# Input contractions of a streaming encoder layer as three products of rounded pairs, with the weights passed through four slots

## The reference

```python
def _layer(x, pool_hist, cache_k, cache_v, cache_kidx, pos0, rel_bias, g_pre, w_in, w_pool, pool_scale, w_out, g_post):
    h = _rmsnorm(x, g_pre)                                   # 1024 channels
    proj = jnp.einsum('bld,de->ble', h, w_in)                # 2600 columns
    u_a, gate_a, q, k, v, qi, ki, wi, gate_b = jnp.split(proj, _SPLITS, axis=-1)
    y_a, new_pool = _pool_mixer(u_a, pool_hist, pos0, w_pool, pool_scale)
    ...
    y_b = _dsa_attention(q, qi, wi, k_all, v_all, ki_all, pos0, rel_bias)   # top-256 keys by indexer score
    mixed = jnp.concatenate([y_a * jax.nn.silu(gate_a), y_b * jax.nn.silu(gate_b)], axis=-1)
    out = jnp.einsum('ble,ed->bld', mixed, w_out)
    return x + _rmsnorm(out, g_post), k, v, ki, new_pool
```

## Time and profile before

| | |
|---|---|
| median of three runs | 1680.02 us |
| span of the profiled execution, first to last instruction | 1677.7 us |
| TensorE busy | 1556.8 us, 93% |
| VectorE busy | 1214.6 us, 72% |
| ScalarE busy | 892.7 us, 53% |
| GpSimd busy | 474.5 us, 28% |
| DMA over the span | 120.76 MB, mean 72 GB/s |

### The profile page before, as it was taken

One profiled execution on the slowest core, in us unless ns is written; L12 is line 12 of the kernel. 1 busy time (PEld: TensorE's weight loads), 2 busy tenths in 40 slices (PEclk: granted clock), 3 DMA queues, 4 the chain that ended last, 5 costly groups with the idle time before them and its releaser, 6 DMA issues.

```text
span 1677.7 us, 17799 instructions
## 1 busy us (share of the span) xinstructions
PE 1556.8 (93%) x5191; PEld 869.7 (52%) x5191; DVE 1214.6 (72%) x2940; ACT 892.7 (53%) x1684; POOL 474.5 (28%) x384
## 2 busy tenths in 40 slices
PE   7999899989999999896988898999999999999996
PEld 4555555555555887663444444444444444455552
DVE  5412578779897566675469999999998999985322
ACT  3112333343334455451498988898988776523331
POOL 0111211121113132303343443434323342322241
PEclk9999999989999999987998999999999999999999
DMA  9322322221112111078324211221220220201011
GB/s 366 74 42 49 80 61 71 56 82 40 61 42 70 48 50 37 35 222 253 81 63 120 80 50 57 59 85 39 61 76 26 52 63 1 63 25 26 32 34 49
DMA packets 91979, 120.76 MB, mean 72 GB/s; under 512 B 17150, under 2 KB 63806, under 8 KB 91499
## 3 DMA queue, kind: packets, MB, share of 16 engines
q1 hardware_dynamic: 90506, 115.44, 22.1%
q10 hardware_dynamic: 1376, 4.19, 2.2%
HBM read 76.06 MB, written 43.54 MB: 71 GB/s over the span
## 4 chain that ended last, share of the span: by engine, by line
PE 23%; DVE 18%; ACT 6%; issue 5%; POOL 2%; POOLq 0%; DVEq 0%; ACTq 0%
PE wide L1648 7%; PE wide L1633 7%; DVE above L345 6%; DVE max_junk L1711 3%; ACT act_junk L1542 2%; PE bank L1613 2%; PE bank L1614 2%; PE bank L1615 2%; PE bank L1618 2%; POOL E L1501 1%; PE bank L1599 1%; DVE den L1727 1%; ACT E L1576 1%; DVE reach L383 1%; DVE S L379 1%
## 5 line engine op out<-in xcount | busy, mean ns | idle before, releaser
L931 PE MATMUL bank<-hT,home 128*128 128x512 f32 (+2 forms) x1280 | 486.1, 516 | 5.1 <-DVE sga L1145 2.4
L1501 POOL TENSOR_TENSOR E<-E,home 128x512 f32<-128x512 f32 (+1 forms) x174 | 251.9, 1452 | 446.8 <-ACT E L1576 446.7
L931 PEld LDWEIGHTS bank<-hT,home 128*128 128x128 f32 x1280 | 234.8, 191 | 165.1 <-issue 144.0
L1576 ACT ACTIVATE E<-bank 128x512 f32<-128x512 f32 (+1 forms) x290 | 165.5, 571 | 245.1 <-PE bank L1618 243.3
L1633 PE MATMUL wide<-E,home 128*128 128x512 f32 x544 | 285.1, 606 | 9.9 <-POOL E L1501 9.7
L907 ACT ACTIVATE relu<-wide 128x1024 f32<-128x1024 f32 (+7 forms) x192 | 153.9, 802 | 216.7 <-PE wide L949 154.5
L1183 DVE SCALAR_TENSOR_TENSOR S<-relu,wi,S 128x1024 f32<-128x1024 f32 (+7 forms) x168 | 173.7, 1034 | 100.1 <-ACT relu L907 92.6
L1711 DVE CUSTOM_DVE_ANT_0 max_junk<-bank,mask 128x512 bf16<-128x512 f32 (+3 forms) x230 | 136.9, 615 | 69.2 <-PE bank L1599 54.6
L1648 PE MATMUL wide<-home 128*128 128x512 f32 x272 | 142.2, 614 | 23.2 <-ACT osb L1568 23.0
L1542 ACT ACTIVATE act_junk<-S,minus_cand 128x1152 bf16<-128x1152 f32 (+5 forms) x105 | 155.4, 1480 | 1.5
L949 PE MATMUL wide<-kiT,qiT 96*128 96x512 f32 (+3 forms) x304 | 139.4, 527 | 6.6 <-ACT relu L907 6.5
(11 more groups left out here) (204 smaller groups left out, 2392.2 us busy)
## 6 DMA issues: line engine op xcount, KB each, us to landing
xs<-x_prompt SPq DMA_DIRECT2D x16, 512.0 KB, 4.5
home<-w_in SPq DMA_DIRECT2D x16, 512.0 KB, 12.8
xr<-x_prompt SPq DMA_DIRECT2D x16, 512.0 KB, 4.2
y_prompt<-osb SPq DMA_DIRECT2D x16, 512.0 KB, 2.9
first_q<-q_high_scratch SPq DMA_DIRECT2D x24, 256.0 KB, 5.0
s_scratch<-S SPq DMA_DIRECT2D x11, 512.0 KB, 2.7
first_q<-q_low_scratch SPq DMA_DIRECT2D x18, 256.0 KB, 4.2
gb<-gb_scratch SPq DMA_DIRECT2D x17, 256.0 KB, 5.3
```

The source lines that it names most:

```text
L931: mm = pe.matmul(out, stationary(c), moving(c), start=(c == 0), stop=(c == DC - 1))
L1501: pool.tensor_tensor(E[:, k % 4, :, 0:n], E[:, k % 4, :, 0:n], EB[:, kv * GRP:(kv + 1) * GRP, off:off + n], ALU.mult)\
L1576: act.activation(E[:, k % 4, :, 0:n], banks[2 + k % 2][:, 0:GRP * n].rearrange("p (j n) -> p j n", j=GRP), ACT.Exp).then_inc(fl_free, 1)
```

## The change

`contract` does three float32r products for each row block instead of one float32 product: every operand x is kept as a pair, HI (x rounded to float32r) and LO (x minus HI), and HI·LO, LO·HI and HI·HI are summed in PSUM.

For that, ScalarE writes the HI half of hT and VectorE subtracts it from the transposed tile in PSUM to give LO; the bank is free after the second. ScalarE's next copy out of banks 0 and 1 waits for VectorE (`low_parts`). ScalarE also scales and rounds the token-major weights, VectorE computes their LO.

The pairs need twice the room, so the 16 groups no longer stay in SBUF. A `ring` of four slots holds a pair each (1 MB). In the first of four token blocks (`SUPERS`: tiles 0-3, 4-7, 8-11, and 16,12,13,14,15) each group is loaded raw (512 KB), scaled on VectorE (WS), rounded on ScalarE (WS), completed on VectorE (WL), and the pair is stored to a DRAM scratch `w_dram`; in each of the other three blocks it is loaded from there (1 MB). A slot's load waits for the end of the contraction that used it before, and in the first block for the slot's store.

The order changes with it: the sample tile comes first in the last block, where each group is used for two sub-blocks of 288 and 256 columns, and the scores are spread evenly over its contractions. TM of a block's first tile moves ahead of the transposes of its fourth tile. The pool windows of the last block are taken once for both sub-blocks, and PL comes two contractions after its window. The first S tile, `wout`, `ma` and `gpost` go into other places of SBUF in phase 2, and two scratch outputs become U8.

```diff
+SUPERS = [(0, (0, 1, 2, 3), (0,)), (4, (4, 5, 6, 7), (1,)), (8, (8, 9, 10, 11), (2,)), (12, (16, 12, 13, 14, 15), (3, 4))]
+SLOTS = 4
+    def split_weights(done):
+        for _ in range(min(done + 3, 16) - (16 - len(raw))):
+            steps.append(("WS", *raw.pop(0)))
+        for _ in range(min(done + 2, 16) - (16 - len(halved))):
+            steps.append(("WL", *halved.pop(0)))
...
+                    if j == 2 and not first:
+                        seek()
+                        project(("TM", t), 3)
...
+    steps += [("H", ST), ("N", 14)]
+    project(("TM", ST), 2)
...
+    steps += [("H", 12), ("N", 15), ("H", 13)]
     spread(100)
+    project(("TM", 12), 0)
...
+    steps += [("H", 14), ("H", 15), ("HIST",)]
...
+                def load_group(n):
+                    slot = n % SLOTS
+                    v, kind, g = fills[n]
+                    if n >= SLOTS:
+                        end = fill_ends[n - SLOTS]
+                        if end in fa:
+                            sp.wait_ge(fa_full, fa[end] + 1)
+                        else:
+                            sp.wait_ge(fg_full, fg[end] + 1)
+                        if n - SLOTS < 16:
+                            sp.wait_ge(wg_out[slot], 16 * ((n - SLOTS) // SLOTS + 1))
+                    if v == 0:
+                        sp.dma_start(raw_group(slot), A["w_in"][:, i * GROUP:(i + 1) * GROUP]).then_inc(wg_in[slot], 16)
+                    else:
+                        sp.dma_start(ring_split[:, slot].rearrange("p a n -> p (a n)").bitcast(F32), w_dram[:, k])\
+                          .then_inc(wg_in[slot], 16)
...
+                    if s in ends_fill and ends_fill[s] + SLOTS < len(fills):
+                        load_group(ends_fill[s] + SLOTS)
...
+                    elif s[0] == "WL":
+                        sp.wait_ge(wg_low, k + 1)
+                        sp.dma_start(w_dram[:, k], ring_split[:, k % SLOTS].rearrange("p a n -> p (a n)").bitcast(F32))\
+                          .then_inc(wg_out[k % SLOTS], 16)
...
+                low_parts = {fa[x] for x in steps if x[0] == "Q"} | {fa["H", t, i] for t in range(NT) for i in range(2)}
...
-                            act.activation(hT[:, 4 * half:4 * half + 4, tt:tt + P],
+                            act.activation(hT[:, HI, 4 * half:4 * half + 4, tt:tt + P],
                                            banks[k % 2][:].rearrange("p (c n) -> p c n", c=4), ACT.Copy)\
-                               .then_inc(fa_free, 1)
+                               .then_inc(h_high, 1)
...
+                    elif s[0] == "WT":
+                            act.activation(wt[:, HI, c, :], wt_raw[:, c, :], ACT.Copy, scale=gpre[:, c:c + 1])\
+                    elif s[0] == "WS":
+                        act.activation(ring_split[:, k % SLOTS, HI], raw_group(k % SLOTS), ACT.Copy).then_inc(wg_high, 1)
...
-                        mm = pe.matmul(out, stationary(c), moving(c), start=(c == 0), stop=(c == DC - 1))
+                        pe.matmul(out, stationary(HI, c), moving(LO, c), start=(c == 0), stop=False)
+                        pe.matmul(out, stationary(LO, c), moving(HI, c), start=False, stop=False)
+                        mm = pe.matmul(out, stationary(HI, c), moving(HI, c), start=False, stop=(c == DC - 1))
...
+                    elif s[0] == "H":
+                        for half in range(2):
+                            dve.wait_ge(h_high, transposed)
+                            dve.tensor_tensor(hT[:, LO, 4 * half:4 * half + 4, tt:tt + P],
+                                              banks[fa["H", t, half] % 2][:].rearrange("p (c n) -> p c n", c=4),
+                                              hT[:, HI, 4 * half:4 * half + 4, tt:tt + P].bitcast(F32), ALU.subtract)\
+                               .then_inc(fa_free, 1)
...
+                    elif s[0] == "WL":
+                        dve.wait_ge(wg_high, k + 1)
+                        dve.tensor_tensor(ring_split[:, k % SLOTS, LO], raw_group(k % SLOTS),
+                                          ring_split[:, k % SLOTS, HI].bitcast(F32), ALU.subtract).then_inc(wg_low, 1)
```

More of the change, by code:

```diff
@@ L24 @@
 I32 = mybir.dt.int32
+U8 = mybir.dt.uint8
 U32 = mybir.dt.uint32
@@ L127, in phase1_steps, with pool_part @@
     windows, short = [], []
-    def pool_part():
-        while windows:
-            steps.append(("PD", *windows[0]))
-            short.append(("PL", *windows.pop(0)))
+    def pool_part(step=None):
+        for window in windows:
+            window[0] -= 1
+        while windows and windows[0][0] == 0:
+            short.extend(("PL", b, g) for b, g in windows.pop(0)[1])
+        if step is not None and step[0] == "U" and step[1] != SUPERS[-1][2][0]:
+            _, b, g = step
+            steps.append(("PD", b, g))
+            windows.append([2, [(x, g) for x in (SUPERS[-1][2] if b == SUPERS[-1][2][1] else (b,))]])
     def transposes(t):
@@ L143, in scores @@
         return [("I", t, h, c) for c in range(len(score_chunks(t))) for h in range(NIH)] if t >= TOPK // P else []
-    for b, (t0, nt) in enumerate(BLOCKS):
-        last = b == len(BLOCKS) - 1
-        ahead = [] if last else list(range(t0 + nt, t0 + nt + min(3, BLOCKS[b + 1][1])))
-        todo = [(k, b, g) for k, g in (LAST_ORDER if last else FIRST_ORDER)]
-        for i in range(nt):
-            t = t0 + i
+    for v, (_, tiles, subs) in enumerate(SUPERS[:-1]):
+        t0, nt, first = tiles[0], len(tiles), v == 0
+        ahead = list(SUPERS[v + 1][1][:3])
+        todo = [(k, subs[0], g) for k, g in FIRST_ORDER]
+        done = 0
+        for i, t in enumerate(tiles):
             if i == 0:
@@ L173, in phase1_steps @@
             for j, step in enumerate(mine):
-                scale(2)
+                if first:
+                    split_weights(done)
                 if step[0] != "Q":
                     seek()
-                project(step, sum(taking[j:]) if taking[j] else 0)
-                pool_part()
-                if step[0] == "U":
-                    windows.append(step[1:])
-                if step in (("GB", len(BLOCKS) - 1, 2), ("GB", len(BLOCKS) - 1, 3)):
-                    steps.append(("NP", step[2] - 2))
+                project(step, sum(v >= 2 or s[0] == "Q" for s in mine[j:]) if v >= 2 or step[0] == "Q" else 0)
+                done += 1
+                pool_part(step)
                 if j == 0:
@@ L205, in phase1_steps @@
                     steps.append(seeking.pop(0))
+    subs = SUPERS[-1][2]
+    todo = [(k, b, g) for g in range(NG) for k in ("U", "GA") for b in subs]
+    todo += [(k, b, g) for g in range(NG) for k in ("GB", "Q") for b in subs]
+    steps += [("H", ST), ("N", 14)]
+    seek()
+    project(("TM", ST), 2)
+    transposes(ST)
+    pool_part()
+    steps += [("H", 12), ("N", 15), ("H", 13)]
     spread(100)
+    seek()
+    project(("TM", 12), 0)
     pool_part()
+    settle()
+    transposes(12)
+    steps += [("H", 14), ("H", 15), ("HIST",)]
+    pending += scores(ST)
+    unscored = [12, 13, 14, 15]
+    for i, t in enumerate((12, 13, 14, 15)):
+        if i:
+            while pending and pending[0][1] == (ST, 12, 13)[i - 1]:
+                spread(1)
+            seek()
+            project(("TM", t), len(todo) + 1)
+            pool_part()
+            transposes(t)
+        for j in range(LAST_SHARES[i]):
+            step = todo.pop(0)
+            if step[0] != "Q":
+                seek()
+            left = len(todo) + 4 - i
+            total = len(pending) + sum(len(scores(u)) for u in unscored)
+            project(step, len(pending) / min(-(-total // left), len(pending)) if pending else 0)
+            pool_part(step)
+            if j == 1:
+                settle()
+                pending += scores(unscored.pop(0))
+            if step in (("GB", subs[1], 2), ("GB", subs[1], 3)):
+                steps.append(("NP", step[2] - 2))
+    spread(100)
+    while windows:
+        pool_part()
     settle()
@@ L1342, in phase2 @@
         vx_set = sem("vx_set")
-        S_in = [loaded["S_in0"], sem("S_in1"), sem("S_in2")]
+        S_in = [sem(f"S_in{i}") for i in range(3)]
         S_used = sem("S_used")
```

358 lines of the change are left out of this document (199 added, 159 removed).

## The result

The changed kernel takes **1749.32 us** (median of 4 runs, 1747.75 to 1750.55) against 1680.14 for the kernel before: a ratio of 1.0412, 95% interval 1.0397 to 1.0426. The forecast was 1654 and faster.

A forecast was written before the change was run, and what follows sets the result against it. TensorE was taken as the bound, with VectorE rising beside it. Terms -104 + 16 + 11.5 + 26 + 19 + 5 = -26.5 gave 1651.2 from the profiled 1677.7, plus 2.3: 1654 us; its own range 1636 to 1670.

The forecast's parts named there:

- start: Before block 0's first projection: rounding, norms and subtractions in series delay it from 25.67 to 41.5 us, +16 us.
- block 0: First block's contractions: cheaper products gain 25 us, nothing given back, since loads and VectorE's subtractions lie beside TensorE.
- block 1 with its start: Second block: 26 us gained, less 5.5 at the boundary and 6 from VectorE and TensorE being level, leaving 14.5.
- block 2 with its start: Third block: VectorE's load and boundary waits give 189 us, so the whole 26 us gain is given back.
- last block with its start: Last five tiles: gain 27 less 19 for TensorE's idle time, first projection 52 us after the block begins; net 8.
- rest, phase 2: Phase 1 ends one weighted sum and store later, +2; TensorE starts cold after gaps, +3; phase 2 zero or 2 us.
- the products: Contractions: three float32r products of 512 columns take 0.695 us against 0.86; gross gain 104 us with the narrow ones.
- Rival 4: Contractions: the operand load does not hide behind running products, +397 us, 2077 us; chance 0.05.
- rival 3: Block 0: the weight feed sets the pace below 275 GB/s; at 201 it adds 64 us, 1718 us; chance 0.17.
- Rivals 1 and 2: Blocks after block 0: TensorE stays the bound, 1624 us, chance 0.16; or VectorE takes all gains, 1676 us, chance 0.14.
- Rival 2: VectorE takes all but block 0; blocks 1, 2 and the last gain nothing, 1676 us; chance 0.14.

The follow-up runs named there:

- e10: e9 with the scaling and rounding of the token-major weights moved after tile 0's transposes instead of after its norm: 1689.07 us.
- e4: Changed kernel with only HI times HI computed, the other two of the three products left out: 1688.16 us.
- e8: Changed kernel with VectorE's weighted sums of the score heads after the first taking only half of the columns: 1718.11 us.
- e1: Changed kernel with the x loads of tiles 7 to 16 issued by ScalarE instead of by SyncE behind its weight loads: 1736.53 us.
- e3: Changed kernel with blocks 1 to 3 loading only 128 of the 2048 columns of each stored pair: 1726.34 us.
- e13: e12 with blocks 1 to 3 loading only 128 of the 2048 columns of each stored pair: 1662.67 us.
- e11: Changed kernel with the norm that waits for a late x tile moved after the transposes of tiles whose x is already there: 1725.86 us.
- e5: Changed kernel where ScalarE's copy of a transposed half no longer waits until VectorE has subtracted the half before: 1739.79 us.
- e12: Changed kernel with all four edits together, those of e1, e2, e5 and e11: 1684.16 us.
- e14: e12 without a search piece ahead of TM of tiles 4, 8, 16 and 12; the pieces come later: 1673.46 us.
- e2: Changed kernel with the last block's contractions ordered U,GA,U,GA and GB,Q,GB,Q over the two sub-blocks instead of U,U,GA,GA: 1722.37 us.
- e15: e14 with tiles 14 and 15 transposed right after norm 15 and two contractions ahead of TM of tile 12: 1669.98 us.
- e9: Changed kernel with the edits of e1, e2 and e5 together: 1687.90 us.

## Why the prediction was wrong

The forecast missed by 1749.3 - 1654 = 95.3 us. By its own steps:

| step | forecast | measured | miss |
|---|---|---|---|
| start | +16 | +16.8 | +0.8 |
| block 0 | -25 | -11.1 | +13.9 |
| block 1 with its start | -14.5 | +1.8 | +16.3 |
| block 2 with its start | 0 | +14.6 | +14.6 |
| last block with its start | -8 | +42.6 | +50.6 |
| rest, phase 2 | +5 | +5.0 | 0 |

(Last block: up to the end of its last contraction at 825.1. The misses add to 96.2; the rounding of the sum and the share outside the span take the other 0.9. The rest agrees partly by luck: 4.1 us lie between the last contraction and phase 2 and 0.9 in phase 2, where the forecast had 2 for the end of phase 1 and 3 for a cold clock.)

- **Right: the products.** 0.69 to 0.70 us for three at 512 columns. Rival 4 is out. By the sentence of the Trainium skill that the prediction cites, in TensorE: Matmul & The Clock Gate (Part 3, "The mechanism"), the operand loads could not have overlapped the products; the starts 0.23 us apart with an operand each say otherwise here as well.
- **Right: the start** (42.5 against 41.5), and along the way: TM of tile 0 starts at 20.1 where 19.7 was forecast. One link of the chain is not needed: e10 shows that ScalarE's rounding ahead of the square sum isn't what decides it.
- **Right in the main: block 2 gives back what the products gain**, and VectorE is why (e4: 5.4 us for two thirds of the products; e8: 10.5 for 13.7 us of VectorE). Its contraction stretch fell by 3.6 us. The rest of its miss is its start.
- **Wrong: "The x load is queued behind a 1 MB weight load ...: +2.5", that the reloads "cost nothing", and "SyncE issues 16 stores and 48 more loads, under 0.5 us each, in idle time".** Most issues do take under 0.5 us, but single ones took 3.9 and 4.1, SyncE waits for stores in the same order, and x was issued 7.6 us late and then landed slowly. The starts of blocks 1 and 2 grew by 17.5 and 18.2 instead of 5.5. e1 shows 6.6 and 6.2 of it; the reload as a whole costs 23.0 us (e3), and 21.5 even with the four edits (e13). The lateness also goes by taking the norm out of the way (e11: 8.1 and 7.7), since it is the order on ScalarE and VectorE that turns a late x of one tile into idle time for the others.
- **Missed: what stands ahead of the new subtraction on VectorE.** I priced a half at 1.4 us in series. The price was right (0.60 and 0.69 us with their hand-overs, and e5's 9.5 us for the order of copies), but the subtraction is on an engine whose queue holds norms, search pieces and weighted sums, and TensorE now waits for it where it had waited for ScalarE. In e12 it stands 10.04 us behind a search piece whose scores are late; without the piece (e14) block 1's start takes 19.6 us, 2.1 less than before the change. In block 2 the piece was worth only 1.3.
- **Wrong: the last block, +19.** Its start took 63.5 us against the 52 added up: the idle time in it was as forecast (26.6 against 28), but TensorE's work took 36.95 us instead of 24, at a granted clock of 0.73. The contraction stretch was 39 us longer than the forecast left for it. I had counted TensorE's work and VectorE's, not that the new order puts two contractions in a row on bank 2: e2 alone gives 27 back. e15 shows that emptying this start pays little by itself (3.5 us).
- **Off in size: block 0, "Nothing given back".** TensorE is idle there for 131.4 - 121.75 = 9.6 us instead of 1.2, in many small waits, and busy for 5.4 us longer than the 116.3 that the forecast left, at a clock of 0.97 instead of 1.00. VectorE waited 15.5 us in this block for raw weights, where the forecast had no such wait, but TensorE waited only 0.9 us for a LO half. The feed (rival 3) wasn't the bound, since e4 goes through the same block in 116.7, at 252 GB/s, where I had asked for 275. Whether it is the feed that stops e4 there wasn't separated.

Rivals 1 and 2 both kept the starts as forecast, and so fell with it. Rival 2 is nearest in where the gain went, nothing kept outside block 0, though only in block 2 mainly by VectorE's load. Rival 3's 1718 is nearest in the time, and that is luck: block 0 missed by 13.9 us and not by 64. With the orders mended, e15 takes 79.3 us off, against the 95.3 missed, with the same products.

What stays open: in block 1's contraction stretch (135.5) neither TensorE's work (e4: 130.4) nor the reload (e3: 130.1) nor VectorE's (e8: 134.6) takes off more than 5.4. TensorE alone needs 129 there, and in e14 the stretch takes 130.0 with TensorE busy for 128.5: what the changed kernel loses above that, 5.5 us, are waits that go with the reload (e3) or with the mended orders (e14). What stands at 130 in e4, when the products are fewer, wasn't separated. Nor was what makes the three edits of e9 more than add, nor what makes an issue of SyncE long.

## What to carry to other kernels

When cheaper matmuls come with a longer preparation, look at where the preparation can't overlap: here TensorE's busy time fell by 62 us, and its idle time grew by 131, more than half of it in the four starts, which no engine's busy share shows. A new step on an engine inherits everything queued ahead of it there, so walk that engine's list, the DMA queue's too, from the step's due time backwards; with those orders mended (e15) the same change is 0.6% faster than the kernel before. And check that two neighbours in a new order don't share the one buffer that the old order kept apart.

## What the runs showed of the hardware

- An issue of a DMA on SyncE takes a median of 0.43 us in phase 1 of the changed kernel, and 3.88 and 4.05 us at 164 and 168 us, at the end of a block in which the DMA engines were busy 75% of the time at 233 GB/s. The load alone doesn't say which issues are long: e3 moves 15/16 less of the reload and has 3.83 us at the same place of the list, and the kernel before, with the engines busy 35% of its block 0, has this one, which the prediction's price left out:

```profile
72.76 4.72 SPq L658 DMA_DIRECT2D gb_scratch<-gst  x1
```

- The granted clock is 0.70 in the starts of blocks 1 and 2, which have TensorE's waits of 17.2 us and the like in them, and 0.99 and 0.94 in the stretches behind them. It stays at 0.73 to 0.75 through the contraction stretches of e4 shown above, so the products that were left there ran below full pace in part of the time. At the lower level, 1.2 GHz, a product of 512 columns starts 0.43 us after the one before, against 0.23. TensorE's timeline in e12, right after the wait of 10.04 us:

```profile
197.55 0.63 PE L1067 MATMUL bank<-hT,ring_split 128*128 128x512 f32 x1
197.98 0.63 PE L1068 MATMUL bank<-hT,ring_split 128*128 128x512 f32 x1
198.41 0.63 PE L1066 MATMUL bank<-hT,ring_split 128*128 128x512 f32 x1
```
